# One core of Trainium2, two trunk layers: 32 instead of 64 moving columns in the RWKV inversion, identity products between its levels, and linear attention's norm at a later place

## The reference, cut to what matters

```python
def step(s, inp):
    r_t, w_t, k_t, v_t, kk_t, a_t = inp
    sa = jnp.einsum('bhvk,bhk->bhv', s, kk_t)
    s = (s * w_t[:, :, None, :] - sa[..., None] * (kk_t * a_t)[:, :, None, :]
         + v_t[..., None] * k_t[:, :, None, :])
    y = jnp.einsum('bhvk,bhk->bhv', s, r_t)
    return s, y
```

```python
o = head_rms_norm(o, NORM_EPS) * lp['gla_gn_g']
out = out + o.reshape(bsz, t, GLA_W) * jax.nn.silu(gd)
```

## Time and profile before

| | us |
|---|---|
| median of 3 runs | 2034.12 (2032.21 to 2042.8) |
| the profiled execution's own time | 2037.5 |
| its span, first to last instruction | 2035.2 |
| PE busy | 1921.4 (94%) |
| DVE busy | 1036.9 (51%) |
| ACT busy | 712.0 (35%) |

### The profile page before, as it was taken

The page is one execution under the profiler, slowest core; times in us unless marked ns, Lnnn a source line. Parts: engine busy times, 40 slices in busy tenths (PEclk is TensorE's granted clock), DMA queues, the critical chain, the costliest instruction groups (busy, mean ns, idle before and its releaser), DMA issues.

```text
span 2035.2 us, 37387 instructions
## 1 busy us (share of the span) xinstructions
PE 1921.4 (94%) x16214; PEld 1730.2 (85%) x16214; DVE 1036.9 (51%) x1627; ACT 712.0 (35%) x1192; POOL 33.8 (2%) x69
## 2 busy tenths in 40 slices
PE   7999999998889899999999999999987889999996
PEld 5899997987679769999979999989756877899996
DVE  2333335655566685333364333466448758533336
ACT  3322223445532343222252222245464225322221
POOL 0000000000000001000000000000000000000000
PEclk9999999998889999999999999999998899899998
DMA  7733336333571045333344333323344004333330
GB/s 324 295 125 126 128 128 236 115 114 124 231 322 45 26 166 187 125 124 124 124 166 145 124 124 124 128 80 124 104 171 174 4 17 152 128 124 124 124 103 31
DMA packets 41471, 277.69 MB, mean 136 GB/s; under 512 B 4778, under 2 KB 6810, under 8 KB 9344
## 3 DMA queue, kind: packets, MB, share of 16 engines
q1 hardware_dynamic: 35424, 255.34, 34.7%
q0 software_dynamic: 3312, 16.91, 2.1%
q10 hardware_dynamic: 2608, 3.56, 0.5%
HBM read 269.22 MB, written 3.41 MB: 134 GB/s over the span
## 4 chain that ended last, share of the span: by engine, by line
PE 81%; DVE 12%; ACT 4%; issue 2%; DMA 1%; PEld 0%; ACTq 0%; PEldq 0%; SPq 0%; POOL 0%; DVEq 0%; POOLq 0%
PE bank L918 17%; PE bank L983 17%; PE bank L922 17%; PE bank L921 17%; PE bank L758 2%; PE bank L1371 1%; DMA ring<-weights 1%; PE bank L1360 1%; PE bank L1378 1%; DVE ring_r L2160 1%; DVE ln_stat L2179 1%; PE bank L839 1%; DVE x L2177 1%; PE bank L767 1%; DVE arena L2170 1%
## 5 line engine op out<-in xcount | busy, mean ns | idle before, releaser
L2160 DVE TENSOR_TENSOR ring_r<-ring,arena_r 128x1024 fp32r<-128x1024 f32 x328 | 387.7, 1221 | 705.9 <-ACT arena_r L1649 705.4
L918 PE MATMUL bank<-arena_r 128*128 128x384 f32 (+3 forms) x2056 | 700.7, 341 | 13.4 <-DVE arena_r L2209 11.3
L922 PE MATMUL bank<-arena_r,ring_r 128*128 128x384 f32 (+2 forms) x1816 | 604.9, 333 | 0.0
L921 PE MATMUL bank<-arena_r 128*128 128x384 f32 (+2 forms) x1816 | 603.1, 332 | 0.0
L918 PEld LDWEIGHTS bank<-arena_r 128*128 128x128 f32 x2056 | 391.7, 191 | 35.4 <-issue 19.9
L1649 ACT ACTIVATE arena_r<-ring 128x1024 fp32r<-128x1024 f32 x340 | 340.4, 1051 | 138.6 <-PE bank L922 136.7
L921 PEld LDWEIGHTS bank<-arena_r 128*128 128x128 f32 x1816 | 343.5, 189 | 3.5
L922 PEld LDWEIGHTS bank<-arena_r,ring_r 128*128 128x128 f32 x1816 | 343.5, 189 | 0.0
L983 PE MATMUL bank<-arena_r 128*128 128x512 f32 x1128 | 310.8, 393 | 0.3 <-issue 0.3
L1780 ACT ACTIVATE arena<-bank 128x384 f32<-128x384 f32 x88 | 43.3, 492 | 739.8 <-PE bank L922 739.8
L983 PEld LDWEIGHTS bank<-arena_r 128*128 128x128 f32 x1128 | 210.7, 188 | 42.2 <-issue 1.2
(11 more groups left out here) (294 smaller groups left out, 1816.8 us busy)
## 6 DMA issues: line engine op xcount, KB each, us to landing
ring<-weights SPq DMA_DIRECT2D x242, 1024.0 KB, 4.9
lnrow<-ln_in POOLq DMA_DIRECT2D x6, 1024.0 KB, 7.0
const<-consts POOLq DMA_DIRECT2D x1, 2211.0 KB, 9.6
arena<-gate POOLq DMA_DIRECT2D x4, 385.0 KB, 8.0
x<-x_in ACTq DMA_DIRECT2D x1, 1536.0 KB, 13.7
rows<-row_in POOLq DMA_DIRECT2D x2, 704.0 KB, 10.5
par<-par_in POOLq DMA_DIRECT2D x2, 662.5 KB, 7.5
y_out<-x SPq DMA_DIRECT2D x2, 512.0 KB, 2.6
```

The source lines that it names most:

```text
L918: mm = pe.matmul(out, w_h, h_h, start=start, stop=False, skip_group_check=True)
L921: pe.matmul(out, w_h, h_l, start=False, stop=False, skip_group_check=True)
L922: return pe.matmul(out, w_l, h_h, start=False, stop=stop, skip_group_check=True)
L2160: ve.tensor_tensor(low_unit((l, name), u) if out is None else out, raw, place.bitcast(F32), ALU.subtract).then_inc(w_ready, 1)
```

## The change

There are three parts. First, every product of levels 1 to 5 moves only the 32 columns that the mask keeps, by a strided view of the 64 (`side`): pieces of w columns, w = 2, 4, 8, 16, 32, read and written with a step of 2w. The stationary operand stays 64x64, and the copies on ACT and DVE stay as they were, over all 512 columns. Second, after each of levels 2 to 5 PE does 6 identity products into bank 7. Third, GLA's norm leaves the end of `gla()` and is done in `rwkv_units`, between DVE's copies of the first and the second group's solved parts; it is now two multiplications of 768 columns and the sum, and `g_o` lies in columns of `mixed` that nobody else uses until then.

```diff
+WARM_LEVEL = 6
...
-        g_o = put(2 * GROUPS * GLA_W).rearrange("p (d g n) -> p d g n", d=2, g=GROUPS)
+        g_o = (mixed[:, :, 256:512], mixed[:, :, 0:256])
...
+                        def side(t, w, upper):
+
+                            return t.rearrange("p (n s w) -> p n s w", s=2, w=w)[:, :, upper, :]
+
+                        def level_products(v, g, bank, kind):
+
+                            w = 1 << v
+                            for d in range(2):
+                                for h, _, _, c in heads_chunks():
+                                    k, o = slice(64 * c, 64 * c + 64), 64 * (4 * d + h)
+                                    x0, x1, low = xz[k, 0, g, d, h, :], xz[k, 1, g, d, h, :], am[k, g, d, h, :]
+                                    got, to = wsb[k, g, o:o + 64], ps[bank][k, o:o + 64]
+                                    if kind == "lx":
+                                        mm = pe.matmul(side(to, w, 1 - d), low, side(x0, w, 1 - d), start=True, stop=True)
+                                    elif kind == "xlx0":
+                                        mm = pe.matmul(side(to, w, 1 - d), x1, side(got, w, 1 - d), start=True, stop=True)
+                                    else:
+                                        mm = pe.matmul(side(to, w, d), got, side(x1, w, d), start=True, stop=True)
+                            return mm
...
-                                        mm = pe.matmul(ps[LX_BANK[g]][k, o:o + 64], am[k, g, d, h, :], xz[k, 0, g, d, h, :],
-                                                       start=True, stop=True)
-                                mm.then_inc(lx_mm, 1)
+                                level_products(v, g, LX_BANK[g], "lx").then_inc(lx_mm, 1)
...
+                            if v > 1:
+                                keep_clock(7, WARM_LEVEL)
...
-                        ve.wait_ge(gla_std, 1)
-                        own.link(ve.reciprocal(gla_ss, gla_ss))
-                        own.link(ve.tensor_tensor(o, o, gla_ss.unsqueeze(2).to_broadcast(heads), ALU.mult))
-                        own.link(ve.tensor_tensor(mixed[:, :, 256:512], g_o[:, 0, :, :], g_o[:, 1, :, :], ALU.add))
...
+                            for d in range(2):
+                                o = g_o[d].rearrange("p g (h n) -> p g h n", h=HEADS)
+                                rate = gla_ss[:, 12 * d:12 * d + 12].rearrange("p (g h) -> p g h", h=HEADS)
+                                own.step(ve.tensor_tensor(o, o, rate.unsqueeze(3).to_broadcast(wide), ALU.mult))
+                            own.settle()
+                            own.link(ve.tensor_tensor(mixed[:, :, 256:512], g_o[0], g_o[1], ALU.add))
...
                         for g, banks in enumerate(((0, 6), (3, 7), (5, 2))):
+                            if g == 1:
+                                gla_norm()
```

More of the change, by code:

```diff
@@ L1356, in rwkv_units @@
                                     pe.wait_ge(inv_ready, n - GROUPS + 1)
-                                for d in range(2):
-                                    for h, _, _, c in heads_chunks():
-                                        k, o = slice(64 * c, 64 * c + 64), 64 * (4 * d + h)
-                                        mm = pe.matmul(ps[LX_BANK[g]][k, o:o + 64], am[k, g, d, h, :], xz[k, 0, g, d, h, :],
-                                                       start=True, stop=True)
-                                mm.then_inc(lx_mm, 1)
+                                level_products(v, g, LX_BANK[g], "lx").then_inc(lx_mm, 1)
                             for g in range(GROUPS):
@@ L1367, in rwkv_units @@
                                     pe.wait_ge(xz_ready, g + 1)
[L1368 to L1373, removed]
-                                if v < RW_LEVELS - 1:
[L1375 to L1380, removed]
+                                level_products(v, g, XLX_BANK[g], "xlx0").then_inc(xlx0_mm, 1)
+                                if v < RW_LEVELS - 1:
+                                    level_products(v, g, LX_BANK[g], "xlx1").then_inc(xlx1_mm, 1)
+                            if v > 1:
+                                keep_clock(7, WARM_LEVEL)
                         def by_token(bank, src, g, done):
@@ L1995, in gla @@
                                 sc.wait_ge(gla_out_mm, 2 * i + d + 1)
-                                sc.activation(g_o[:, d, ORDER[d][i], :], ps[2 * (i % 2) + d][:, 0:GLA_W],
+                                sc.activation(g_o[d][:, ORDER[d][i], :], ps[2 * (i % 2) + d][:, 0:GLA_W],
                                               ACT.Copy).then_inc(gla_out_read, 1)
@@ L1999, in gla @@
                             for d in range(2):
-                                sc.activation(g_sq[:, d, ORDER[d][i], :], g_o[:, d, ORDER[d][i], :],
+                                sc.activation(g_sq[:, d, ORDER[d][i], :], g_o[d][:, ORDER[d][i], :],
                                               ACT.Square).then_inc(gla_squared, 1)
@@ L2550, in summed @@
                                                           g_sq[:, d, g, :].rearrange("p (h n) -> p h n", h=HEADS), AX, ALU.add))
-                                own.step(ve.tensor_tensor(g_o[:, d, g, :], g_o[:, d, g, :], gd[:, d, g, :], ALU.mult))
+                                own.step(ve.tensor_tensor(g_o[d][:, g, :], g_o[d][:, g, :], gd[:, d, g, :], ALU.mult))
                         own.step(ve.tensor_scalar(ka1, prm("k_a"), -1.0, 1.0, ALU.mult, ALU.add))
@@ L2590, in gla @@
                         ve.tensor_tensor(sw[1][:, :, WIN], high[:, :, WIN], sw[1][:, :, WIN], ALU.subtract).then_inc(cum_ready, 1)
-                        heads = [P, 2 * GROUPS * HEADS, 64]
-                        o = g_o[:, :, :, :].rearrange("p d g (h n) -> p (d g h) n", h=HEADS)
-                        ve.wait_ge(gla_std, 1)
-                        own.link(ve.reciprocal(gla_ss, gla_ss))
-                        own.link(ve.tensor_tensor(o, o, gla_ss.unsqueeze(2).to_broadcast(heads), ALU.mult))
-                        own.link(ve.tensor_tensor(mixed[:, :, 256:512], g_o[:, 0, :, :], g_o[:, 1, :, :], ALU.add))
                         ve.wait_ge(gla_out_read, 2 * GROUPS)
@@ L2655, in first, with gla_norm @@
                                                am[:, g, :, :, :]).then_inc(xz_ready, 1)
+                        def gla_norm():
+                            wide = [P, GROUPS, HEADS, 64]
+                            ve.wait_ge(gla_std, 1)
+                            own.link(ve.reciprocal(gla_ss, gla_ss))
+                            for d in range(2):
[4 more added lines that the diff above has]
+                            own.link(ve.tensor_tensor(mixed[:, :, 256:512], g_o[0], g_o[1], ALU.add))
                         ve.wait_ge(xz_filled, 2)
```

## The result

The changed kernel takes 2069.03 us (median of 4 runs, 2063.44 to 2081.5) against 2035.46 for the kernel before, measured again beside it (4 runs, 2032.21 to 2042.8). The ratio is 1.0168, interval 1.0133 to 1.0202. The forecast was slower, and it is slower, but by 33.6 us in place of 11.7, outside the stated range of 2026 to 2060. The profiled execution is the shortest of the four: 2063.44 us, span 2061.1, 25.9 more than before.

What follows compares the result with a forecast made beforehand. PE was taken to bound the inversion, running its levels without a pause. Identity products 12.2, columns 0, norm -0.7 and +0.2 made 11.7 us slower, 2034.1 to 2045.8 us; range 2026 to 2060, about 8 in 10.

Steps and rivals of the forecast that it cites:

- Step 1: Inversion levels on PE: weight columns set the pace, so 32 moving columns gain 0, at most 6.7 us.
- The first rival: Levels' products: moving columns set the pace, a group takes 0.467 us, kernel 23.5 us faster at 2010.6; chance 0.11.
- the second (load after load): Levels' products: load and stream run in turn, 0.70 us a group, kernel 7.9 us faster at 2026.2; chance 0.06.
- Step 2: Identity products after levels 2 to 5: 6.12 us per layer, 12.2 us in two layers, nothing hides them.
- Step 3: The norm's move on DVE: 0.7 us gained at the old place in layer 1, 0.2 lost at the new one.
- the sum of 11.7: Whole kernel: 12.2 for identity products, 0 for columns, -0.7 and +0.2 for the norm, 11.7 us slower.
- the rival "the clock falls": Levels with 32 columns: granted clock halves, 8.4 us per level; 2054 if in one layer, 2063 in both; chance 0.10.

Runs made afterwards that it cites:

- e10: The kernel before with only the 32 moving columns added, norm at its old place, no identity products: median 2041.7 us over 12 runs.
- e7: Changed kernel with 32x32 tiles in levels 1 to 4, level 5 at 64x64 with 64 columns, no identity products: 2102.3 us, 1.0321 times the kernel before.
- e11: Changed kernel with 32x32 tiles in level 5 only, 64 columns in the other levels, no identity products: 2034.6 us, 0.9987 times the kernel before.
- e1: Changed kernel with 64 moving columns put back, identity products and the norm's new place kept: 2047.5 us, 1.0031 times the kernel before.
- e3: Changed kernel with 64 moving columns and no identity products, leaving only the norm's new place: 2036.0 us, 0.9982 times the kernel before.
- e5: Changed kernel with 64 moving columns in level 1 only, 32 elsewhere, no identity products: 2035.5 us, 0.9992 times the kernel before.
- e6: Changed kernel with identity products only in level 1's two pauses, two in each, none after the levels: 2034.8 us, 0.9992 times the kernel before.

## Why the prediction was wrong, by its own steps

*Step 1, 32 columns change nothing at full clock: right.* The groups of layer 0 take 0.94 us, and e10's undisturbed runs equal the kernel before. The reason given, that the weights set the pace, rests on the earlier trace rows; e7 and e11 fit it, and e11 puts the supply of instructions aside. The first rival (columns set the pace) and the second (load after load) would have shown 0.47 and 0.70. Pieces of 2 columns, for which no row existed, cost nothing either: level 1's groups with such pieces take 0.93 in layer 0 (620.92 to 621.85). The rule of the Trainium skill, Advanced Engine Details and Errata, PSUM Cachelines, that pieces slow a matmul, isn't borne out in a time here: a stream twice as long would hide behind the weight load.

*Step 2, the blocks cost 12.2 us: right within a microsecond.* 11.5 between e1 and e3, and 6.5 a layer in e1's trace against 6.12. That layer 0 of the changed kernel shows 5.9 is partly luck: a level with its block is 10.06 - 8.40 = 1.66 longer where 1.60 was taken, level 5 is 1.47 longer where 1.32 was, 6.45 in all, and the 0.5 us that PE waits for DVE in level 1 of layer 0 before are missing there.

*Step 3, the norm, -0.7 and +0.2: right* as far as the trace goes (0.7 less in layer 1; `inner` 0.5 late in layer 0 where 0.4 was the most, caught up by the end of the stage).

So the sum of 11.7 was right for what it summed: e1, in which the clock holds, reads 2047.5 where 2045.8 was forecast, and of the 33.6 us about a third is what the forecast meant by "slower". *What failed is that the forecast put the clock at nothing, 1.00 in all levels, and with it the chance and the price of the rival "the clock falls".* It had 0.10, on the ground that a stretch with the same half stream had kept the clock. That stretch had no pauses; level 1 has two, and the text looked for the columns' effect in the levels at large and not at their entry. And it was priced at one level at half clock, 8.4 us. Measured are 47.8 us at half clock, some 22 us lost: once fallen, the clock came back neither with the groups nor, in this execution, with the first block of 12 instructions. The rival's own warning, that a busy PE is no sign that the clock stays, was in the text; it was given a chance of 0.10, and 8.4 us where 22 were lost. Why the same columns and pauses bring the fall in one execution and not in another stays open.

Nothing here beats the kernel before by more than can be measured: e3, e5, e6 and e11 all include 1 in their intervals.

## What to carry to other kernels

Halving the moving columns of a product gained nothing here, where 64 weight columns were loaded for each: look for two rows that differ in one of the two before counting columns. What such an edit does change is how much PE streams while it is "busy", and here that was paid where PE also pauses: ask of the entry of a stage, not of its middle, whether the clock survives, and price a fall by how long the stage may offer nothing to end it (30.7 to 71.7 us in these traces). Products that are to hold the clock belong into the pauses, where they cost 0.6 us a layer (e6), not behind work that has none.

## What the runs showed of the chip that I had not expected

- The same program falls in some executions and not in others: eight of e10's twelve at 2029.6 to 2042.3, four at 2069.0 to 2072.9. A median over both says little; the list of single times says it.
- At half clock a group of 64x64 with 32 columns takes 1.71 us, 1.83 times its 0.93.
- With 32x32 tiles PE stands still for 1.4 to 2.6 us behind bursts of 8.5 to 9.2 ns a matmul and comes to 72 instructions a us (e7), where the 64x64 levels of before need 67. A limit in the supply of instructions fits this; no run shows it alone.
- The clock falls or holds with the same instructions and the same two pauses, even within one execution (e10, layers 0 and 1).
